# Reordering the end of the first stage: convolution chain ahead of attention on every engine, and the second turning of heads inside the output product

## The reference, cut to what matters

```python
# token_mixer(h, ...): q, k, v, qi, ki, wi, gate_b, gate_c, hc = split(h @ w_in)
attn = sparse_indexer_attention(q, k, v, qi, ki, wi, k_sel).reshape(bsz, s, ATTN_WIDTH)   # softmax(q k) v, 8 heads of 64
attn = group_rms_norm(attn, attn_norm_g, N_HEADS_ATTN)

u = gate_c * hc
u_pad = jnp.pad(u, ((0, 0), (CONV_K - 1, 0), (0, 0)))
conv = sum(conv_w[j] * u_pad[:, j:j + s, :] for j in range(CONV_K))                        # three taps
conv_out = group_rms_norm(gate_b * conv, conv_norm_g, CONV_GROUPS)                         # 8 groups of 64

mixed = jnp.concatenate([attn, conv_out], axis=-1)
return mixed @ w_out
```

## Time and profile before

| what | us |
|---|---|
| median of 3 runs | 1451.31 (1450.16 to 1457.05) |
| the profiled execution's own time | 1458.36 |
| its span in the trace | 1456.7 |
| TensorE busy | 1413.5 (97% of the span) |
| VectorE busy | 1051.5 (72%) |
| ScalarE busy | 705.6 (48%) |
| GpSimd busy | 184.4 (13%) |
| mean granted TensorE clock | 0.981 of full |

### The profile page before, as it was taken

The page is one execution under the profiler, slowest core; times in us unless marked ns, Lnnn a source line. Parts: engine busy times, 40 slices in busy tenths (PEclk is TensorE's granted clock), DMA queues, the critical chain, the costliest instruction groups (busy, mean ns, idle before and its releaser), DMA issues.

```text
span 1456.7 us, 19791 instructions
## 1 busy us (share of the span) xinstructions
PE 1413.5 (97%) x7136; PEld 1182.1 (81%) x7136; DVE 1051.5 (72%) x1105; ACT 705.6 (48%) x936; POOL 184.4 (13%) x272
## 2 busy tenths in 40 slices
PE   8998899999999999999999999999999999899998
PEld 8897788888788877767788887788888988788887
DVE  5888867776768877676667775688866888665555
ACT  2453353434643335666734345534338856544342
POOL 3103211110301110221101101111101000100000
PEclk7996999999999999999999999999999999999999
DMA  9836478996489994532589983899955332466661
GB/s 356 319 140 203 146 257 296 314 313 234 141 297 343 373 358 161 189 125 93 192 270 314 314 280 115 287 335 339 343 181 190 116 129 87 129 203 223 225 228 58
DMA packets 187527, 335.62 MB, mean 230 GB/s; under 512 B 9170, under 2 KB 123454, under 8 KB 187217
## 3 DMA queue, kind: packets, MB, share of 16 engines
q1 hardware_dynamic: 160528, 237.95, 48.8%
q0 software_dynamic: 26736, 96.71, 18.3%
q10 hardware_dynamic: 208, 0.23, 0.0%
HBM read 332.23 MB, written 2.63 MB: 230 GB/s over the span
## 4 chain that ended last, share of the span: by engine, by line
PE 78%; DVE 10%; issue 4%; ACT 4%; DMA 3%; POOL 1%; ACTq 0%; DVEq 0%; SPq 0%; POOLq 0%
PE ps L2155 67%; DVE wlo L1294 2%; DMA raw<-in_ffn_w_in 2%; PE ps L2349 1%; PE ps L2610 1%; PE ps L2163 1%; POOL st L494 1%; PE ps L2280 1%; ACT whi L674 1%; DVE ada_acc L1627 1%; PE ps L2149 1%; DVE xn L1356 1%; PE ps L2294 1%; ACT hf L699 1%; DVE xs L1361 1%
## 5 line engine op out<-in xcount | busy, mean ns | idle before, releaser
L1294 DVE TENSOR_TENSOR wlo<-raw,whi 128x2048 fp32r<-128x2048 f32 x203 | 463.4, 2285 | 146.3 <-ACT whi L674 145.1
L2155 PE MATMUL ps<-whi,hhi 128*128 128x512 f32 (+1 forms) x1208 | 490.3, 406 | 14.0 <-DVE hlo L1347 4.6
L674 ACT ACTIVATE whi<-raw 128x2048 fp32r<-128x2048 f32 x208 | 396.3, 1909 | 218.7 <-PE ps L2155 163.1
L2155 PE MATMUL ps<-whi,hlo 128*128 128x512 f32 (+1 forms) x1208 | 475.0, 393 | 0.0
L2155 PE MATMUL ps<-wlo,hhi 128*128 128x512 f32 (+1 forms) x1208 | 474.0, 392 | 0.0
L2155 PEld LDWEIGHTS ps<-whi,hhi 128*128 128x128 f32 x1208 | 229.5, 190 | 67.4 <-issue 8.3
L2155 PEld LDWEIGHTS ps<-whi,hlo 128*128 128x128 f32 x1208 | 228.9, 189 | 49.5
L2155 PEld LDWEIGHTS ps<-wlo,hhi 128*128 128x128 f32 x1208 | 229.9, 190 | 45.0 <-issue 1.7
L2155 PE MATMUL ps<-whi,ahi 128*128 128x512 f32 x400 | 156.2, 390 | 0.7 <-DVE alo L1514 0.7
L2155 PE MATMUL ps<-whi,alo 128*128 128x512 f32 x400 | 155.7, 389 | 0.0
L2155 PE MATMUL ps<-wlo,ahi 128*128 128x512 f32 x400 | 155.7, 389 | 0.0
(11 more groups left out here) (288 smaller groups left out, 1495.6 us busy)
## 6 DMA issues: line engine op xcount, KB each, us to landing
raw<-in_ffn_w_in SPq DMA_DIRECT2D x176, 512.0 KB
ada_raw<-in_ada_w POOLq DMA_DIRECT2D x96, 512.0 KB, 5.2
raw<-in_ffn_w_down SPq DMA_DIRECT2D x44, 1024.0 KB
big<-in_ada_w POOLq DMA_DIRECT2D x48, 512.0 KB, 6.1
raw<-in_hgrn_w_in SPq DMA_DIRECT2D x16, 1024.0 KB
raw<-in_attn_w_qkv SPq DMA_DIRECT2D x12, 1024.0 KB
ada_raw<-in_w_ada POOLq DMA_DIRECT2D x23, 512.0 KB, 4.9
raw<-in_w_gate SPq DMA_DIRECT2D x22, 512.0 KB
```

The lines of the kernel that those rows point to most:

```text
L674: sc.activation(whi[:, slot, 0:n], raw[:, slot, 0:n], ACT.Copy).then_inc(w_hi, 1)
L1294: ve.tensor_tensor(wlo[:, slot, 0:n], raw[:, slot, 0:n], whi[:, slot, 0:n].bitcast(F32), ALU.subtract)\
L2155: done = pe.matmul(dst, lhsT, rhs, start=first and n == 0, stop=final and n == 2, skip_group_check=True)
```

## The change

In words, queue by queue:

- **ScalarE:** the four scalings of the convolution go ahead of `take_turned(0)`, and each signals conv_tap; `take_turned(1)` goes ahead of the convolution's square; `hi(U+12)` and the copy of the turned roots go ahead of `square_heads_out(1)`.
- **VectorE:** pieces 7 and 8 move to either side of `logits(1)`, ahead of conv_u; the taps of each block wait for its own scaling; `pt_evac(1)` stands ahead of piece 9; `heads_out(1)` moves behind the convolution's mixing, `heads_norm(1)` behind the first turned heads; `lo(U+12)` moves between the second turned heads and their split; pieces 12 to 20 are placed anew.
- **GpSimd:** one more piece is loaded ahead of the first root; each later one moves up by one accordingly.
- **TensorE:** `turn_weights(1)` goes ahead of `attend(0)`; `attend(1)` is cut in two around the transposes of the roots; the fillers of 5 and 7 go, those of 8 become 22; the second transposes of heads move into the output product, between unit U+10 and unit U+11; the wait for mix_f 3 and the gate's sums move from ahead of U+11 to ahead of U+12.

```diff
--- before.py
+++ after.py
@@ -606,17 +606,17 @@
                     pool.wait_ge(f_used, 13)
                     pool.wait_ge(w_hi, 2)
                     pool.wait_ge(cols_sum, 1)
-                    for n in range(13):
+                    for n in range(14):
                         early_piece(n)
                     pool.wait_ge(block_mean, 1)
                     inverse_root(st[:, 40:56], 16, block_root)
-                    early_piece(13)
+                    early_piece(14)
                     pool.wait_ge(block_mean, 2)
                     inverse_root(st[:, 120:128], 8, block_root)
-                    early_piece(14)
+                    early_piece(15)
                     pool.wait_ge(block_mean, 3)
                     inverse_root(st[:, 128:136], 8, block_root)
-                    for n in range(15, EARLY):
+                    for n in range(16, EARLY):
                         early_piece(n)
                 elif s == 1:
 
@@ -1238,21 +1238,20 @@
             exps(0)
             hi(U + 11)
             exps(1)
-            take_turned(0)
             sc.wait_ge(conv_u, 1)
             sc.wait_ge(w_used, used(U + 7))
             for ct in range(4):
-                done = sc.activation(hf[:, ct, :], big[:, D + ct * TOK:D + (ct + 1) * TOK], ACT.Copy,
-                                     scale=vec[:, V_CW + 8 + ct:V_CW + 9 + ct])
-            done.then_inc(conv_tap, 1)
+                sc.activation(hf[:, ct, :], big[:, D + ct * TOK:D + (ct + 1) * TOK], ACT.Copy,
+                              scale=vec[:, V_CW + 8 + ct:V_CW + 9 + ct]).then_inc(conv_tap, 1)
+            take_turned(0)
             square_heads_out(0)
+            take_turned(1)
             sc.wait_ge(conv_gated, 1)
             sc.activation(hfl[:, 0:D], hfl[:, D:2 * D], ACT.Square).then_inc(conv_sq, 1)
-            take_turned(1)
-            square_heads_out(1)
             hi(U + 12)
             sc.wait_ge(group_tr, 1)
             sc.activation(act[0:8, 0, 0:TOK], ps[0:8, 1, 0:TOK], ACT.Copy).then_inc(group_out, 1)
+            square_heads_out(1)
             split_mixed(1, 4, 4, 0, TOK)
             for t in range(NT):
                 split_mixed(2 + t, 0, 4, t * P, P)
@@ -1746,56 +1745,61 @@
             choose(1)
             logits(0)
             lo(U + 9)
+            early_piece(7)
             logits(1)
+            early_piece(8)
             ve.wait_ge(w_used, used(U + 9))
             ve.wait_ge(hc_out, 1)
             ve.tensor_tensor(big[:, D:2 * D], big[:, 0:D], bank(2, 2), ALU.mult).then_inc(conv_u, 1)
-            early_piece(7)
             lo(U + 10)
-            early_piece(8)
-
-            ve.wait_ge(conv_tap, 1)
+
             for ct in range(4):
+                ve.wait_ge(conv_tap, ct + 1)
                 for j in (1, 2):
                     w = V_CW + 4 * (2 - j) + ct
                     link(ve.scalar_tensor_tensor(cv[:, ct, j:TOK], u[:, ct, 0:TOK - j], vec[:, w:w + 1], cv[:, ct, j:TOK],
                                                  ALU.mult, ALU.add))
             ve.tensor_tensor(hfl[:, D:2 * D], hfl[:, 0:D], bank(0, 2), ALU.mult).then_inc(conv_gated, 1)
+            pt_evac(1)
             early_piece(9)
-            pt_evac(1)
-            early_piece(10)
             ve.wait_ge(group_mm, 1)
             ve.tensor_scalar(st[:, 40:56], ps[:, 0, 0:16], 1.0 / 64, EPS1, ALU.mult, ALU.add).then_inc(block_mean, 1)
             heads_out(0)
+            early_piece(10)
             early_piece(11)
             lo(U + 11)
-            early_piece(12)
-            heads_out(1)
             heads_norm(0)
-            early_piece(13)
-            heads_norm(1)
 
             ve.wait_ge(spread_mm, 1)
             for ct in range(4):
                 done = ve.scalar_tensor_tensor(hf[:, 4 + ct, :], hf[:, 4 + ct, :], vec[:, V_CG + ct:V_CG + ct + 1],
                                                psf[:, ct * TOK:(ct + 1) * TOK], ALU.mult, ALU.mult)
             done.then_inc(mix_f, 1)
-            early_piece(14)
+            heads_out(1)
             split_mixed(1, 4, 4, 0, TOK)
-            for t in range(NT):
+
+            def turned_heads(t):
+
                 ve.wait_ge(o_tr, t + 1)
                 ve.tensor_tensor(hf[:, 0:4, t * P:(t + 1) * P], ps[:, 4 + t, :].rearrange("p (k n) -> p k n", k=4),
                                  vec[:, V_AG:V_AG + 4].unsqueeze(2).to_broadcast((P, 4, P)), ALU.mult).then_inc(mix_f, 1)
-                split_mixed(2 + t, 0, 4, t * P, P)
+
+            turned_heads(0)
+            early_piece(12)
+            split_mixed(2, 0, 4, 0, P)
+            heads_norm(1)
+            early_piece(13)
+            turned_heads(1)
+            lo(U + 12)
+            split_mixed(3, 0, 4, P, P)
+            early_piece(14)
+            early_piece(15)
+            lo(U + 13)
             ve.wait_ge(lam_exp, 1)
             link(ve.tensor_tensor(st[:, 220:221], st[:, 219:220], st[:, 218:219], ALU.subtract))
             link(ve.tensor_scalar(st[:, 221:222], st[:, 220:221], -LAMBDA_INIT, None, ALU.add))
-            lo(U + 12)
-            for n in range(15, 19):
+            for n in range(16, 21):
                 early_piece(n)
-            lo(U + 13)
-            early_piece(19)
-            early_piece(20)
             leave_first()
 
             def attention():
@@ -2319,7 +2323,7 @@
                         pe.wait_ge(mix_lo, mixed_ready[j, t])
 
                 def before(j, t):
-                    if s == 0 and (j, t) == (0, 0):
+                    if s == 0 and (j, t) == (1, 0):
                         pe.wait_ge(mix_f, 3)
                         sum_gate(0)
                     mixed(j + 1, t)
@@ -2816,15 +2820,12 @@
                                             logit_rows(t)[:, h, g * P:(g + 1) * P], ident)
                 done.then_inc(p_tr, 1)
 
-            def attend(t):
-                pe.wait_ge(pt_s, t + 1)
-                if t:
-                    pe.wait_ge(pt_v, 1)
-                for h in range(HEADS):
+            def attend(t, heads):
+                for h in heads:
                     for g in range(t + 1):
                         done = pe.matmul(ps[:, (2, 6)[t], h * 64:(h + 1) * 64], PT[:, g, h * P:(h + 1) * P],
                                          tok[:, g, VO:VO + 64], start=g == 0, stop=g == t)
-                done.then_inc(pv_mm, 1)
+                return done
 
             pe.wait_ge(qT_out, 1)
             logit_products(0)
@@ -2837,10 +2838,10 @@
             keep_busy(4, 4)
             pe.wait_ge(conv_u, 1)
             turn_weights(0)
-            keep_busy(5, 5)
-            attend(0)
             turn_weights(1)
-            keep_busy(8, 3)
+            pe.wait_ge(pt_s, 1)
+            attend(0, range(HEADS)).then_inc(pv_mm, 1)
+            keep_busy(22, 3)
 
             pe.wait_ge(conv_sq, 1)
             for t in range(NT):
@@ -2848,22 +2849,31 @@
                     done = pe.matmul(ps[:, 0, 8 * t + 2 * ct:8 * t + 2 * ct + 2], hf[:, ct, t * P:(t + 1) * P],
                                      kc[:, C_HALF:C_HALF + 2], start=True, stop=True)
             done.then_inc(group_mm, 1)
-            attend(1)
+            pe.wait_ge(pt_s, 2)
+            pe.wait_ge(pt_v, 1)
+            attend(1, range(4))
             pe.wait_ge(block_root, 1)
             for t in range(NT):
                 done = pe.transpose(ps[0:8, 1, t * P:(t + 1) * P], st[:, 40 + 8 * t:48 + 8 * t], ident)
             done.then_inc(group_tr, 1)
-            keep_busy(7, 3)
+            attend(1, range(4, HEADS)).then_inc(pv_mm, 1)
             pe.wait_ge(group_out, 1)
             pe.wait_ge(spread_land, 16)
             for ct in range(4):
                 done = pe.matmul(psf[:, ct * TOK:(ct + 1) * TOK], gate[0:8, 1, ct * P:(ct + 1) * P], act[0:8, 0, 0:TOK],
                                  start=True, stop=True)
             done.then_inc(spread_mm, 1)
-            for t in range(NT):
+
+            def turn_heads_out(t):
                 pe.wait_ge(o_done, t + 1)
                 transposes([big[:, 3920 + BANK * t + j * P:3920 + BANK * t + (j + 1) * P] for j in range(4)], 4 + t, o_tr)
-            output_product(0, U + 10, {(0, 0): 1, (2, 0): 2, (2, 1): 3}, 4)
+
+            def beside_first(j, t):
+                if (j, t) == (1, 0):
+                    turn_heads_out(1)
+
+            turn_heads_out(0)
+            output_product(0, U + 10, {(0, 0): 1, (2, 0): 2, (2, 1): 3}, 4, beside_first)
 
             for s in range(1, NSUB):
                 if s in SWIGLUS:
```

## The result

| | before | changed |
|---|---|---|
| median, us | 1455.89 (1450.16 to 1461.11, 10 runs) | 1460.02 (1457.98 to 1463.79, 10 runs) |
| profiled execution, us | 1458.36 | 1459.76 |
| its span, us | 1456.7 | 1457.1 |

The ratio is 1.0042 with a 95% interval of 1.0028 to 1.0056, taken between runs of the two kernels in the same rounds, so the changed kernel is slower by 4.1 to 8.2 us, 6.1 in the middle. A later measurement gave 1.0042 again (1.0029 to 1.0055). The medians of the table alone lie 4.1 us apart; those of the kernel before in later rounds were lower than its 1455.89: 1454.2 to 1454.5, each of 21 to 35 runs.

What follows compares the result with a forecast made beforehand. The stage's end was taken as the later of output product and VectorE's last piece, which gains only by less idling. Last piece +2.4 and column sums +1.6 gave +4.0 on 1451.3: 1455.3 us, range 1447 to 1460.

Steps and rivals of the forecast that it cites:

- 1451.3 + 4.0: Whole kernel: median level 1451.3 us plus 4.0 us of loss in the stage, giving 1455.3 us.
- column sums: TensorE at the stage's end: after standing 5 us the 32 sums start at low clock, costing 1.6 us more.
- the tail is unchanged: Everything behind the column sums: the change doesn't touch it, so nothing is added to the +4.0 us.
- rival (c): Clock returns late in the product's first unit (+3.1) and column sums (+2.0 more): +9.1 us, 1460.4; chance 0.12.
- Part 1: Convolution ahead of the group sums: taps 2.4 us earlier, but fillers eat it; sums start at 119.95 against 120.00.
- Parts 2 and 3: GpSimd's root to the output product: spread done at 132.8 against 137.13, product starts at 137.1, 4.1 us earlier.
- Part 4: VectorE during the output product: waits 3.4 us for the second transposes of heads; its last piece comes 2.4 us later.
- (a): TensorE's clock stays high from 119.95 to the product: -1.0 us, 1450.3; chance 0.20.
- (b): TensorE's gain carries through because VectorE stands less than summed: -4.1 us, 1447.2; chance 0.12.

Runs made afterwards that it cites:

- e9: The changed kernel again, unchanged, for a second profile and more rounds; ratio 1.0042 to the kernel before, columns read 67.7 us after the first transposes of weights.
- e6: Kernel before with only the late turning of heads: second transposes behind U+10, gate's sums ahead of U+12; ratio 1.0057 to the kernel before.
- e1: Changed kernel plus 20 filler calls between the output product and the column sums; ratio 1.0019 to the kernel before, sums 3.84 us.
- e2: Changed kernel with the second transposes of heads between the halves of U+10 instead of behind both; ratio 1.0019 to the kernel before.
- e8: The kernel before again, unchanged, for a second profile; column sums took 3.84 us, columns read 61.5 us after the first transposes of weights.
- e5: Kernel before with 20 filler calls instead of 8 ahead of the group sums; ratio 0.9990 to the kernel before.
- e7: Changed kernel with 12 fillers ahead of the group sums, second transposes between U+10's halves, pieces placed in VectorE's waits; ratio 1.0000 to the kernel before.

## Why the prediction was wrong, and where it was right

**The number.** 1460.02 lies just above the range's end of 1460. The step that failed is the last one of the sum, "1451.3 + 4.0", in both its terms.

The level: three runs gave 1451.31; ten give 1455.89, and the larger sets 1454.2 to 1454.5, so it was 3 to 4.6 us too low. Runs of one kernel spread over 11 us here, so a median of three was worth 3 or 4 us either way, and I gave that no share of the range. The profiled execution, 1458.36, had pointed the other way.

The step: +4.0 stands against +6.1 (4.1 to 8.2) by the ratio. That the two medians of ten lie 4.1 apart, as forecast, is luck. One term is shown to be too small, that of the column sums (below). Another was put at nothing, "the tail is unchanged": in both profiles of the changed kernel the next stage's 60 matmuls took 13.9 us and not 15.4, which gave 1.5 us back. What brings the stage's +2.6 and +4.6 us at their end up to 6.1 in the whole is open (below).

The range, too: it was to reach up to rival (c), whose own sum was 1460.4, and it was closed at 1460, below it.

**Part 1.** Right: the taps came 1.9 us earlier in absolute time, 2.4 from the stage's start (2.07 after the first transposes, for 4.46), and the fillers ate it. The group sums start 10.9 us after the first transposes, as before.

**Parts 2 and 3.** Right within 0.8 us, and early: the spread was read 23.0 us after the first transposes and the product started at 27.3, where my 132.85 and 137.1 were 23.8 and 28.1. The clock lasted longer than I took it to: it was 1.00 up to 126 and 0.59 at 126 to 128, after TensorE had stood 1.45 us for the root. In e9 that half of attend(1) ran low and the spread was read at 23.7.

**Part 4.** Right: 3.36 us of waiting for 3.4 (4.24 in e9, 5.81 for 5.8 in e6). The last piece was to come 2.4 us later; it came 1.6 later in one profile and 3.1 in the other.

**The column sums.** Undersized: 1.6 us more were forecast (by its own figures, 5.3 less 3.84, 1.5), 2.5 and 2.9 measured, and e1 shows by itself that the clock is worth these 2.5. I had let the clock rise after 3.15 us, as it did at 141.21. Here it stayed at 0.50 from 168 to 174 and rose only towards the end of the 32.

**Rivals.** (a), the clock that stays high through everything, is refuted: 0.50 from 128 to 140. (b) is refuted by the measured time, and e2 and e6 show why: VectorE's wait for the second transposes sets the end. Of (c), the late return of the clock, a part came true. For the column sums it had 2.0 us more than my sum, and 0.9 and 1.3 were measured; for the first unit of the product it had 3.1 more, and that unit took 7.07 us in the first profile (7.12 forecast) and 7.93 in e9.

In the three profiles in which TensorE stood 2.92 us ahead of the group sums (before, e8, e6) these took 2.93 to 3.57 us; in the nine others, where the gap was filled, 1.84 to 1.95. The rule of the Trainium skill ("TensorE: Matmul & The Clock Gate", section on HAM oscillation), that gaps drop the clock, agrees with this. The rule does not fit what came next: in e5 the clock fell again between 121 and 122, inside attend(1), though TensorE had not stood longer than 0.30 us since 108.4. There the measurement decides.

**What stays open.** Against the kernel before, the ratios lie 1 to 4 us above what the profiles show for the stage (e2: 2.8 us slower by the ratio, 1.0 faster by the stage; e7: the same, and 2.4 faster; e5 alone agrees). This need not be a loss elsewhere. The two profiled executions of the kernel before took 1458.36 and 1460.04 us, 4 and 6 above the medians of its rounds, while those of the other kernels lie from 2 below to 3 above theirs. So the stage's time that all are compared with may come from executions that took longer than most. With one or two profiles for each kernel neither is shown.

## What to carry to other kernels

Ask which engine's last instruction releases the next stage, and add up that engine's waits; a chain made shorter on another engine gains only what those waits lose (1.5 us of waits and 1.6 at the end in e5). A wait put into a full in-order queue costs its own length and whatever stands behind it, here conversions of weights that TensorE then stands for. And an engine that becomes early has to be kept busy in the right place: fillers in front of a late release gave 2.5 us in the stage, while those that outlasted their release held the group sums back by 2.2 us, of which 0.7 reached the stage's end.

## What the hardware showed that I had not expected

TensorE's low clock came with little idle time, and not alike in executions of the same code. In the changed kernel it fell at 126 to 127, behind fillers, 16 group sums of 2 columns, half of attend(1) and one wait of 1.45 us; in e5 it fell inside attend(1) with no wait over 0.30 us for 13 us.

It came back as unevenly. In the kernel before it stayed at 0.50 from 121 to 144, although TensorE was busy without a gap from 120.0 to 139.0. In e6, with the same instructions up to the spread, it was at 0.50 from 117 on but back at 1.00 by 131 to 132, during the fillers of 128x128. Elsewhere it was back 3.2 us after a product of 128x512 had started, and 5 us after the column sums had. So a low clock taken from one profile is not a property of the code alone.

GpSimd's roots of 8 columns took 2.78 and 1.67 us before, and 1.99 and 2.56 in the changed kernel, the same two roots beside other work of VectorE. The other profiles show the same two pairs, by which of the two orders they have. A price of such a root taken from a row with other neighbours can be off by 0.8 or 0.9 us.
